# A two-block transformer kernel: narrower level matmuls, five reordered steps, and weight tiles placed 64 bytes further on

## The chip, the cores and the metric

One Trainium2 chip, one of its cores. The metric is the device time of one execution in microseconds (us). The kernel before takes 3259.83 us, the median of three runs (3259.44 to 3262.21).

## The reference, cut to what matters

256 tokens (`T`) of width 2048 (`D`) pass through four layers, all in float32. Each layer begins with a norm over the width and ends with a product that is added to the stream.

```python
x = hgrn2_layer(...)    # stage A, OA: h @ w_in (2048 x 8192), gated linear recurrence with 16 heads of 128,
                        #   head norm, silu gate, @ w_out
x = fox_layer(...)      # stage FG, F, OF: keys, values, queries, gate from 2048-wide products, causal softmax
                        #   with a forget bias, head norm, silu gate, @ w_out
                        # second block, stage X, C, OC:
proj = rmsnorm(x) @ w_in          # recurrence input, queries, latent keys/values, index queries and keys, 2 gates
y_rnn  = rg_lru(causal_conv(xr))  # per-channel linear recurrence
y_attn = dsa_attention(...)       # per query the 64 best keys by an index score, then softmax over them
x = x + (sigmoid(gr) * y_rnn + sigmoid(ga) * y_attn) @ w_o
                        # stage Q, U0..U3, V0..V3: a product-key expert layer over all 16384 experts
act = gelu(x @ u.T) * gate        # gate is zero but for the 128 chosen experts of a token
x = x + act @ v
return rmsnorm(x)
```

In the recurrence of stage A the mask inside a 128-token block is built from seven levels: at level l the block falls into pairs of halves of h = 2^l tokens, and the second half of each pair (queries) meets the first half (keys).

## The kernel before, in words

Everything is one program with a hand-written order on each engine. A weight matrix is cut into *units* of 128 output columns: one DMA of 1 MB from the SP queue into one of four `raw` slots, ScalarE copies it in two halves to `wh` (rounded to the fp32r format, L1049), VectorE writes `raw - wh` over `raw` as `wl` (`low_half`, `low_part`, L1512). TensorE then does 48 matmuls for a unit (`product`, L518 to L520): for each of 16 slices k the weights `wh[k]` against the high part `hh[k]` and the low part `hl[k]` of the stream, and `wl[k]` against `hh[k]`. In these the weight slice (128 columns, 512 bytes in a partition) is the *stationary* operand and the slice of the stream (256 columns, 1024 bytes) the *moving* one. In the profile's names the moving operand stands first: `bank<-hh,wh`. Keys and values of stage F use `kh` and `kl` in place of `hh` and `hl`.

In the value stages V0 to V3 it is the other way round: `ah` and `al`, the high and low parts of the activations, are stationary and the weights move, 512 columns at a time (L1018 to L1020). In stage C two small products use `uk_h`, `uk_l` as stationary and `ckv_h`, `ckv_l` as moving (L868 to L870), right after them `ckv` as stationary and `uv_h`, `uv_l` as moving (L876 to L878).

SBUF tensors are laid out one after another, each rounded up to 32 bytes. From the shapes the start addresses within a partition come out as follows (bytes): `hh` 16384, `hl` 32768, `kh` 141312, `ckv_h` 145408, all multiples of 1024; `wl` 49216 and `wh` 81984 onwards in steps of 8192, all 64 past a multiple of 1024; `uk_h` 153664 is 64 past one, `uv_h` 161984 is 192 past one; `ah` 194368 and `al` are 832 past one (320 past a multiple of 512).

The steps that the change touches:
- `a_levels` (L664 to L684) issues on TensorE for each of the seven levels four float32 matmuls of 128 stationary columns (`KL[l]`) by 64 moving columns (the second halves of `QL[l]`); the profile shows each float32 matmul as two. `a_masks` on VectorE (L1718 to L1738) takes the wanted squares out of PSUM into `AT`, with four masked copies per level.
- `out_projection` (L604) with `products_in_flight` (L579 to L602) begins the output products of a stage while the last head pair is still being finished: `count` units are computed up to slice 13, and at given points (unit, slice) the work of the last pair is put in: `f_values` (weigh the values) and `f_norm` (the head norm's sum, which waits for `osq_f` from ScalarE). The last two slices of those units come at the end. A raw slot is given back only when its unit is complete.
- In stage X VectorE sums the index scores of 16 heads (L1896) and in between splits weights (`low_part`).
- In the first head pair of stage C `select` (four rounds of max and replace) is called twice around the step that reads `ri_read`.
- `v_turns(2)` (stage V2) runs on VectorE for each unit: `act_low` (the low part of the activations for the next unit), two `low_half`, `gate` for the next block, and after the 16th and 32nd unit `add_experts`, which adds four PSUM banks to the stream. TensorE waits for these adds before it reuses a bank.

Of the kernel before, what the change touches and what calls it, by code (L numbers as in the profile page):

```python
# [24 lines left out]
P = 128  # L25
D = 2048
T = 256
KC = D // P
NT = T // P
# [6 lines left out]
LEVELS = 7  # L36
SC = P + T
# [12 lines left out]
BJ = 32  # L50
# [50 lines left out]
def program(nc, x_fm, prm_h, f_bias_h, w_in_a, w_out_a, w_fgate, w_kv, w_in_b, w_out_b, w_latent, w_ikey, w_iquery, w_in_c,  # L101
            rg_wa, rg_wx, w_uk, w_uv, w_out_c, w_q, keys1, keys2, peer_u, peer_v, fin_h, out):
    ctx = ExitStack()
    with ctx:
# [14 lines left out]
        qw = sb("qw", [P, 1])  # L119
        m = ExitStack()  # L120
# [12 lines left out]
        spare = sb("spare", [P, 16])  # L133
# [193 lines left out]
        frstd = sb_in(m, "frstd", [P, 40])[:, 0:NT]  # L327
# [180 lines left out]
        def _(eng):  # L508
# [155 lines left out]
            def a_levels(i):  # L664
# [9 lines left out]
                for l in range(LEVELS):  # L674
                    h = 1 << l
                    bank, at = (B[5 + l // 2], (l % 2) * T) if l < 6 else (B[3], 0)
                    if l == 6:
                        eng.wait_ge(s["gate_read"], i + 1)
                    for n in range(2 * NT):
                        last = eng.matmul(bank[:, at + n * (P // 2):at + (n + 1) * (P // 2)], KL[l][:, n * P:(n + 1) * P],  # L680
                                          halves(QL[l][:, n * P:(n + 1) * P], h)[:, :, 1, :], start=True, stop=True)
# [97 lines left out]
            out_projection("OF", "F", "C", 2, {(0, 6): (f_values,), (0, 12): (f_norm,)})  # L779
# [728 lines left out]
        def _(eng):  # L1508
# [209 lines left out]
            def a_masks(i, first, end):  # L1718
# [9 lines left out]
                for l in range(first, end):  # L1728
                    h, nb = 1 << l, P >> (l + 1)
                    bank, at = (B[5 + l // 2], (l % 2) * T) if l < 6 else (B[3], 0)  # L1730
                    dst = AT[:, :, :].rearrange("p n (b two r) -> p n b two r", two=2, r=h)[:, :, :, 1, :]
# [4 lines left out]
                    last = eng.drain()  # L1736
                if end == LEVELS:
                    last.then_inc(s["at_ready"], 1)  # L1738
# [148 lines left out]
            low_part(0, u + 9)  # L1887
            for n in range(IDX_HEADS):
                if n % 4 == 0 and n // 4 < 3:
                    low_part(0, u + 10 + n // 2)  # L1890
                    low_part(0, u + 11 + n // 2)
# [40 lines left out]
            def c_body(i, first, final=False):  # L1932
# [23 lines left out]
                low_part(i, u + 5)  # L1956
                if first:
                    select(TOPK // 16)
                eng.wait_ge(s["ri_read"], i + 1)
# [210 lines left out]
            def v_turns(b):  # L2170
# [4 lines left out]
                for n in range(BJ):  # L2175
# [4 lines left out]
                    if more:  # L2180
                        low_half(0, u, 0)
                    if gating:
                        gate(b + 1, 0, n, (b + 1, 0, n + 2) if n + 2 < BJ else None)
# [4 lines left out]
                    if n % (BJ // 2) == BJ // 2 - 1:  # L2188
                        add_experts(b, n // (BJ // 2))
# [106 lines left out]
```

## Time and profile before

| | |
|---|---|
| median of 3 runs | 3259.83 us (3259.44 to 3262.21) |
| the profiled execution's own time | 3263.68 us |
| its span in the trace | 3261.9 us |
| TensorE matmul busy | 3224.8 us, 99% |
| weight load busy | 3061.1 us, 94% |
| VectorE busy | 2334.3 us, 72% |
| ScalarE busy | 1656.7 us, 51% |
| granted TensorE clock, mean | 0.997 |
| DMA | 569.95 MB, mean 175 GB/s |

The span is the time from the first to the last instruction in the trace of one execution. A matmul's duration there includes its way through the array, so consecutive matmuls overlap; what a matmul costs in a stream is the distance from start to start, which is called *pitch* below.

### The profile page before, as it was taken

The page shows a single profiled execution, that of the slowest core. Times are in us where ns is not written, and L with a number is a line of the kernel's source. Part 1 is how long each engine was busy: PE and PEld are TensorE (multiplying, and loading weights), DVE is VectorE, ACT ScalarE, POOL GpSimd, SP SyncE. Part 2 cuts the span into 40 slices and gives each one's busy share as a digit, 9 for nine tenths or more (in the row PEclk, how much of TensorE's full clock was granted, in tenths as well). Part 3 has the DMA queues.
Part 4 walks back from the last instruction along what each step waited for, and adds up shares of the span by engine and source line. Part 5 has one row for each costly group of instructions (what it writes and reads, how often), then busy time and mean ns, then how long its engine had stood idle before and what let it go on. Part 6 is the DMA issues. An engine that isn't in the chain of part 4 may idle for free.

```text
span 3261.9 us, 62833 instructions
## 1 busy us (share of the span) xinstructions
PE 3224.8 (99%) x25256; PEld 3061.1 (94%) x25256; DVE 2334.3 (72%) x3775; ACT 1656.7 (51%) x2215; POOL 7.5 (0%) x27
## 2 busy tenths in 40 slices
PE   8999999999999999999999999999999999999998
PEld 7999999999999999999999999998899889987887
DVE  7767666654555676666668998985698658999865
ACT  5454544767674555656544434444444444444444
POOL 0000000000000000000000000000000000000000
PEclk9999999999999999999999999999999999999999
DMA  5444435444444455454555455555555555555554
GB/s 183 142 167 143 166 131 180 168 156 166 155 167 168 168 182 173 163 187 164 176 183 180 172 192 181 182 190 194 187 186 184 191 193 184 181 181 181 181 206 155
DMA packets 99095, 569.95 MB, mean 175 GB/s; under 512 B 9456, under 2 KB 30320, under 8 KB 31600
## 3 DMA queue, kind: packets, MB, share of 16 engines
q1 hardware_dynamic: 98928, 567.58, 49.6%
q8 instruction: 122, 2.00, 0.2%
q14 instruction: 45, 0.37, 0.0%
HBM read 565.45 MB, written 2.10 MB: 174 GB/s over the span
## 4 chain that ended last, share of the span: by engine, by line
PE 89%; DVE 8%; DVEq 1%; ACT 1%; issue 0%; DMA 0%; ACTq 0%; SPq 0%
PE bank L518 21%; PE bank L519 20%; PE bank L520 20%; PE bank L1018 6%; PE bank L1020 6%; PE bank L1019 6%; DVE wl L1512 2%; PE bank L680 2%; PE bank L944 1%; PE bank L622 1%; DVE hot_a L2096 1%; DVEq L2115 1%; PE bank L858 0%; PE bank L743 0%; PE bank L742 0%
## 5 line engine op out<-in xcount | busy, mean ns | idle before, releaser
L518 PE MATMUL bank<-hh,wh 128*128 128x256 f32 x5696 | 1612.0, 283 | 10.2 <-DVE hl L1545 9.0
L519 PE MATMUL bank<-hl,wh 128*128 128x256 f32 x5696 | 1582.6, 278 | 0.0
L520 PE MATMUL bank<-hh,wl 128*128 128x256 f32 x5696 | 1582.5, 278 | 0.0
L1512 DVE TENSOR_TENSOR wl<-raw,wh 128x1024 fp32r<-128x1024 f32 x1052 | 1253.8, 1221 | 413.7 <-ACT wh L1049 405.8
L1049 ACT ACTIVATE wh<-raw 128x1024 fp32r<-128x1024 f32 x1052 | 1052.1, 1050 | 316.2 <-DMA raw<-w_in_a 135.8
L518 PEld LDWEIGHTS bank<-hh,wh 128*128 128x128 f32 x5696 | 1074.0, 189 | 22.2 <-issue 12.5
L519 PEld LDWEIGHTS bank<-hl,wh 128*128 128x128 f32 x5696 | 1073.7, 189 | 7.3 <-issue 6.9
L520 PEld LDWEIGHTS bank<-hh,wl 128*128 128x128 f32 x5696 | 1073.3, 188 | 0.0
L1018 PE MATMUL bank<-wh,ah 128*128 128x512 f32 x1024 | 402.0, 393 | 1.3 <-DVE xT L2161 1.3
L1020 PE MATMUL bank<-wl,ah 128*128 128x512 f32 x1024 | 398.9, 390 | 0.0
L1019 PE MATMUL bank<-wh,al 128*128 128x512 f32 x1024 | 398.6, 389 | 0.0
L1018 PEld LDWEIGHTS bank<-wh,ah 128*128 128x128 f32 x1024 | 192.3, 188 | 40.8 <-DVE xT L2161 1.7
L1020 PEld LDWEIGHTS bank<-wl,ah 128*128 128x128 f32 x1024 | 192.2, 188 | 40.8
L1019 PEld LDWEIGHTS bank<-wh,al 128*128 128x128 f32 x1024 | 192.4, 188 | 39.1
L2096 DVE TENSOR_TENSOR hot_a<-iota_h,slotT 128x1024 f16<-128x1024 f16 x128 | 156.0, 1219 | 0.0
L518 PE MATMUL bank<-kh,wh 128*128 128x256 f32 x496 | 141.2, 285 | 0.0
L520 PE MATMUL bank<-kh,wl 128*128 128x256 f32 x496 | 138.4, 279 | 0.0
L519 PE MATMUL bank<-kl,wh 128*128 128x256 f32 x496 | 138.4, 279 | 0.0
L1464 ACT ACTIVATE ah<-act 128x512 fp32r<-128x512 f32 x64 | 40.4, 631 | 179.0 <-PE bank L1020 179.0
L2122 DVE TENSOR_TENSOR al<-act_odd,ah 128x512 fp32r<-128x512 f32 x64 | 44.3, 693 | 120.5 <-ACT ah L1464 120.5
L1449 ACT ACTIVATE act_odd<-bank 128x256 f32<-128x256 f32 (+1 forms) x64 | 24.6, 384 | 205.7 <-PE bank L520 205.7
L1464 ACT ACTIVATE ah<-act_odd 128x512 fp32r<-128x512 f32 x64 | 40.4, 632 | 173.0 <-PE bank L1020 171.8
(364 smaller groups left out, 2849.4 us busy)
## 6 DMA issues: line engine op xcount, KB each, us to landing
raw<-peer_u SPq DMA_DIRECT2D x128, 1024.0 KB, 4.9
raw<-peer_v SPq DMA_DIRECT2D x128, 1024.0 KB, 4.9
raw<-w_in_c SPq DMA_DIRECT2D x64, 1024.0 KB, 4.9
raw<-w_in_a SPq DMA_DIRECT2D x63, 1024.0 KB, 4.9
raw<-w_kv SPq DMA_DIRECT2D x32, 1024.0 KB, 4.9
raw<-w_in_b SPq DMA_DIRECT2D x32, 1024.0 KB, 4.9
raw<-w_out_a SPq DMA_DIRECT2D x16, 1024.0 KB, 5.0
raw<-w_out_b SPq DMA_DIRECT2D x16, 1024.0 KB, 4.9
```

The source lines that it names most:

```text
L518: eng.matmul(out, h_[:, k, :], high[:, k, :], start=(k == 0), stop=False)
L519: eng.matmul(out, h_[:, k, :], low[:, k, :], start=False, stop=False)
L520: last = eng.matmul(out, low_rows(c, k), high[:, k, :], start=False, stop=(k == KC - 1))
L680: last = eng.matmul(bank[:, at + n * (P // 2):at + (n + 1) * (P // 2)], KL[l][:, n * P:(n + 1) * P], halves(QL[l][:, n * P:(n + 1) * P], h ...
L1018: eng.matmul(bank[:, :], a_h, w_h, start=first, stop=False)
L1019: eng.matmul(bank[:, :], a_l, w_h, start=False, stop=False)
L1020: last = eng.matmul(bank[:, :], a_h, w_l, start=False, stop=final)
L1049: eng.activation(high_half(c, half), raw_half(c, half), ACT.Copy).then_inc(hi_ready, 1)
L1464: eng.activation(ah[c % 2][:, :, :], acts[b % 2][:, 2 * c:2 * c + 2, :], ACT.Copy).then_inc(s["ah_ready"], 1)
L1512: eng.tensor_tensor(low_half_out(c, half), raw_half(c, half), high_half(c, half).bitcast(F32), ALU.subtract).then_inc(lo_ready, 1)
L2096: eng.tensor_tensor(hot_a[c % 2][:, :, :], iota_h[:, :].unsqueeze(1).broadcast_to(ka), slotT[:, 0, tt].unsqueeze(2).broadcast_to(ka), ALU. ...
L2122: eng.tensor_tensor(al[c % 2][:, :, :], acts[b % 2][:, 2 * c:2 * c + 2, :], ah[c % 2][:, :, :].bitcast(F32), ALU.subtract).then_inc(s["al_ ...
```

## The change

It has seven edits. `NARROW = 5`: levels 5 and 6 of `a_levels` use only the columns that are wanted. `spare` moves in front of `raw`: `wl` and all `wh` start 64 bytes later, at 128 past a multiple of 1024; `iota`, `prm`, `ident` and `ones` move with them, and from `tri` on every address is as before. `frstd` gets 16 more floats: `ah`, `al` and what follows start 64 bytes later too, at 896 past a multiple of 1024 (384 past a multiple of 512). The other four change the order of work.

```diff
+NARROW = 5
@@ addresses
+        spare = sb("spare", [P, 16])        # now ahead of raw, wl, wh
-        spare = sb("spare", [P, 16])        # was behind rg_c
-        frstd = sb_in(m, "frstd", [P, 40])[:, 0:NT]
+        frstd = sb_in(m, "frstd", [P, 56])[:, 0:NT]
@@ a_levels, TensorE
                     for n in range(2 * NT):
-                        last = eng.matmul(bank[:, at + n * (P // 2):at + (n + 1) * (P // 2)], KL[l][:, n * P:(n + 1) * P],
-                                          halves(QL[l][:, n * P:(n + 1) * P], h)[:, :, 1, :], start=True, stop=True)
+                        if l < NARROW:
+                            eng.matmul(...)      # as before
+                        else:
+                            for a in range(0, P, 2 * h):
+                                eng.matmul(bank[a:a + h, at + n * (P // 2) + a // 2:at + n * (P // 2) + a // 2 + h],
+                                           KL[l][:, n * P + a:n * P + a + h], QL[l][:, n * P + a + h:n * P + a + 2 * h], start=True, stop=True)
@@ a_masks, VectorE
+                    if l >= NARROW:
+                        level = bank[:, at:at + T].rearrange("p (n t) -> p n t", n=2 * NT)
+                        for a in range(0, P, 2 * h):
+                            eng.tensor_copy(AT[a:a + h, :, a + h:a + 2 * h], level[a:a + h, :, a // 2:a // 2 + h])
+                        continue
@@ TensorE, end of stage F
-            out_projection("OF", "F", "C", 2, {(0, 6): (f_values,), (0, 12): (f_norm,)})
+            out_projection("OF", "F", "C", 3, {(0, 6): (f_values,), (1, 0): (f_norm,)})
@@ VectorE, stage X
+            lows_at = {0: (10, 11), 4: (12, 13), 8: (14,), 12: (15,)}
             for n in range(IDX_HEADS):
-                if n % 4 == 0 and n // 4 < 3:
-                    low_part(0, u + 10 + n // 2)
-                    low_part(0, u + 11 + n // 2)
+                for c in lows_at.get(n, ()):
+                    low_part(0, u + c)
@@ VectorE, first pair of stage C
-                low_part(i, u + 5)
                 if first:
                     select(TOPK // 16)
+                low_part(i, u + 5)
@@ VectorE, v_turns
+                    if gating and n == BJ // 2 - 1:
+                        add_experts(b, 0)
                     if gating:
                         gate(b + 1, 0, n, (b + 1, 0, n + 2) if n + 2 < BJ else None)
...
-                    if n % (BJ // 2) == BJ // 2 - 1:
+                    if n == BJ - 1 or n == BJ // 2 - 1 and not gating:
                         add_experts(b, n // (BJ // 2))
```

## Rows read from the trace of the kernel before

**Rows 1.** The page: span, and each engine's busy us, share of the span, instructions.

```profile
span 3261.9 us, 62833 instructions
PE 3224.8 (99%) x25256; PEld 3061.1 (94%) x25256; DVE 2334.3 (72%) x3775; ACT 1656.7 (51%) x2215; POOL 7.5 (0%) x27
```

**Rows 2.** Stretches of 30 us: each engine's busy us (instructions), clock, DMA share, GB/s.

```profile
1010.00:1040.00 30.00, 30.00 (x257) 30.00 (x256) 18.13 (x23) 12.89 (x15) 0.00 (x0) 1.00 0.56 199
1640.00:1670.00 30.00, 30.00 (x267) 30.00 (x266) 17.92 (x23) 11.99 (x14) 0.00 (x0) 1.00 0.52 179
```

**Rows 3.** Groups by line, count | busy us, mean ns: 1010 to 1040, 1640 to 1670, whole run.

```profile
L519 PE MATMUL bank<-hl,wh 128*128 128x256 f32 x86 | 24.2, 281 | 0.0
...
L519 PE MATMUL bank<-hl,wh 128*128 128x256 f32 x89 | 24.6, 276 | 0.0
...
L519 PE MATMUL bank<-hl,wh 128*128 128x256 f32 x5696 | 1582.6, 278 | 0.0
```

**Rows 4.** Timeline of TensorE, a later pair of stage C: start, duration.

```profile
1253.44 0.28 PE L870 MATMUL bank<-ckv_h,uk_l 128*128 128x256 f32 x1
...
1255.91 0.28 PE L870 MATMUL bank<-ckv_h,uk_l 128*128 128x256 f32 x1
...
1256.27 0.28 PE L878 MATMUL bank<-uv_h,ckv_l 128*128 128x256 f32 x1
...
1258.77 0.28 PE L518 MATMUL bank<-hh,wh 128*128 128x256 f32 x1
...
1259.47 0.28 PE L518 MATMUL bank<-hh,wh 128*128 128x256 f32 x1
```

**Rows 5.** A 30 us stretch of stage V0, matmuls of L1019 alone.

```profile
2200.00:2230.00 30.00, 17.15 (x45) 8.27 (x45) 1.00 0.58 206
```

**Rows 6.** Timeline of TensorE: the levels of one head pair; one gate turn, f16.

```profile
77.50 6.36 PE L680 MATMUL bank<-QL,KL 128*128 128x64 f32 x56
...
2101.22 0.41 PE L944 MATMUL bank<-gates_b,hot_a 128*128 128x64 f16 x8
```

**Rows 7.** Timeline of TensorE around index scores, which use 64 of 128 rows.

```profile
1166.79 0.28 PE L520 MATMUL bank<-hh,wl 128*128 128x256 f32 x1
1167.00 1.69 PE L807 MATMUL bank<-kiT,qi 64*128 64x128 f32 x16
1168.62 0.39 PE L518 MATMUL bank<-hh,wh 128*128 128x256 f32 x1
```

**Rows 8.** Timeline of TensorE, starts of OA and OF: waits in brackets.

```profile
489.49 0.39 PE L518 MATMUL bank<-hh,wh 128*128 128x256 f32 x1 [0.43 <-DVE wl L1512]
...
993.70 1.13 PE L622 MATMUL bank<-osq_f,ones 128*128 128x512 f32 x2 [0.75 <-ACT osq_f L1240]
...
1000.83 0.38 PE L588 MATMUL bank<-hh,wh 128*128 128x256 f32 x1 [0.35 <-DVE hl L1570]
```

**Rows 9.** Timeline of VectorE and TensorE, stage X and first pair of stage C.

```profile
1168.79 2.36 DVE L1512 TENSOR_TENSOR wl<-raw,wh 128x1024 fp32r<-128x1024 f32 x2 [6.00 <-ACT wh L1049]
1171.24 6.77 DVE L1896 SCALAR_TENSOR_TENSOR iscore<-relu,kw,iscore 128x128 f32<-128x128 f32 x16
...
1184.35 2.76 DVE L1950 SCALAR_TENSOR_TENSOR xc<-bank,prm,xc 128x255 f32<-128x255 f32 x6
...
1191.89 2.36 DVE L1512 TENSOR_TENSOR wl<-raw,wh 128x1024 fp32r<-128x1024 f32 x2 [2.28 <-ACT wh L1049]
...
1187.41 1.03 PE L858 MATMUL bank<-xc,wa 128*128 128x256 f32 x4
...
1221.15 0.87 PE L628 MATMUL bank<-ident,prob_c 128*128 128x128 f32 x6 [2.70 <-DVE prob_c L1816]
```

**Rows 10.** Timeline of VectorE and TensorE, middle of stage V2.

```profile
2979.83 0.42 DVE L2111 SCALAR_TENSOR_TENSOR g_sum<-bank,g_low 128x256 f32<-128x256 f32 x1
...
2983.87 2.48 DVE L2161 TENSOR_TENSOR xT<-bank,xT 128x512 f32<-128x512 f32 x4
...
2984.61 0.50 PE L1018 MATMUL bank<-wh,ah 128*128 128x512 f32 x1 [1.29 <-DVE xT L2161]
```

More of the change, by code:

```diff
@@ L679, in a_levels @@
                     for n in range(2 * NT):
-                        last = eng.matmul(bank[:, at + n * (P // 2):at + (n + 1) * (P // 2)], KL[l][:, n * P:(n + 1) * P],
-                                          halves(QL[l][:, n * P:(n + 1) * P], h)[:, :, 1, :], start=True, stop=True)
+                        if l < NARROW:
+                            eng.matmul(bank[:, at + n * (P // 2):at + (n + 1) * (P // 2)], KL[l][:, n * P:(n + 1) * P],
+                                       halves(QL[l][:, n * P:(n + 1) * P], h)[:, :, 1, :], start=True, stop=True)
+                        else:
+                            for a in range(0, P, 2 * h):
+                                eng.matmul(bank[a:a + h, at + n * (P // 2) + a // 2:at + n * (P // 2) + a // 2 + h],
+                                           KL[l][:, n * P + a:n * P + a + h], QL[l][:, n * P + a + h:n * P + a + 2 * h], start=True, stop=True)
                 for j in range(2):
@@ L1735, in a_masks @@
                                             .rearrange("p (b r) -> p b r", r=h))
-                    last = eng.drain()
+                    eng.drain()
                 if end == LEVELS:
-                    last.then_inc(s["at_ready"], 1)
+                    eng.drain().then_inc(s["at_ready"], 1)
             def a_body(i, first):
```

## The prediction

> **What bounds the kernel now.** I read the page first. TensorE's matmuls cover 99% of the span and VectorE 72% [rows 1], so a microsecond counts only where TensorE waits or where its own work gets shorter or longer. The list of waits then showed that TensorE waits little: a few places of 0.5 to 3 us, three of which the change aims at [rows 8 to 10]. So the rest is the pitch of a matmul, and there the stretches of 30 us show something unexpected. Both stretches hold nothing but the same three lines at the same granted clock, 1.00 (the 2.4 GHz level), with the DMA and VectorE doing nearly the same, but one has 257 matmuls and the other 267 [rows 2]. About 2.4 of each count are matmuls that only reach into the stretch, so the pitch is 30/254.6 = 117.8 ns in the one and 30/264.6 = 113.4 ns in the other. I call them long and short pitch. The groups show the same as a duration: 281 ns in the stretch of 257, 276 in that of 267, 278 over the whole run [rows 3]. So some (278-276)/5 = 2/5 of these matmuls go at the long pitch (3/10 to 5/10 with the rounding). There are 5696 of each of three lines with `hh`, and 496 more of each with `kh`, together 18,576. At the long pitch: 7,400, at 4.4 ns, so it costs 33 us of the span (25 to 41). Matmuls at the short pitch: 11,100.
>
> Is it a matter of addresses, which the change moves? One place speaks for it [rows 4]. In stage C the key product (stationary 64 past a multiple of 1024, moving on one) goes at (1255.91-1253.44)/21 = 117.6 ns; then without a pause the value product (stationary on a multiple of 512, moving 192 past one of 1024) at (1258.77-1256.27)/22 = 113.6 ns; then, again without a pause, the ordinary product (64 past, and on one) at (1259.47-1258.77)/6 = 117 ns. The switch follows the operands. Against it: ordinary products with the very same placement also go at the short pitch in one of the two stretches of rows 2. So the placement of 64 allows both, and something else, the timing at which a run of matmuls is entered, chooses. The new placement of 128 occurs nowhere in this trace.
>
> **The change part by part.** Against the profiled execution: 3263.68 us, of which the span is 3261.9.
>
> *Narrow levels.* Levels 5 and 6 are 16 of the 56 records in 6.36 us [rows 6], less about 0.16 us for the last one's way out: 0.111 us each, 1.77 us a pair. After it there are 8 matmuls of 32 by 32 columns and 4 of 64 by 64, which makes 16 + 8 = 24 records, and three changes of the array's shape. No row shows a matmul with fewer than 128 stationary columns. Upper end: each of the 24 costs 0.111 as now, 2.66. Lower end: 0.030 each, the start-to-start of the f16 matmuls (eight within 0.41 us, the last one's 0.19 included) [rows 6], 0.72. The nearest shape change is that to 64 rows and back: 1167.00-1166.79 is 0.21 where 0.12 is usual, and the first product behind it lasts 0.39 instead of 0.28 [rows 7]. So some 0.1 each way; three are 0.3, and 0.6 if such a change costs double. Between the ends I take 0.03 for the 16 and 0.055 for the 8, half of 0.111 for half the columns: 0.48 + 0.44 + 0.5 = 1.42, a gain of 0.35 a pair and 2.5 us over eight pairs, rounded down. Ends: 0.72 + 0.3 (1.02 a pair) gives -6 us, 2.66 + 0.6 (3.26) gives +12. VectorE's masks get about 1 us shorter a pair, beside TensorE: nothing. The Trainium skill ("TensorE: Matmul & The Clock Gate", LDWEIGHTS) has the load time go with the column count, and "TensorEngine Tiling (Array Packing)" (Key Properties) says that a change of the tiling mode drains the array; the first alone would be an estimate of 27 ns a load for 32 columns, hence 16 x 0.027 + 8 x 0.053, a gain of 0.9 us a pair before the drains. No row here has such a load.
>
> *Start of OF.* The head norm waits 0.75 us for `osq_f`, and the last pair's `hl` another 0.35, about 0.5 with the issue behind it [rows 8]. Now six more matmuls lie ahead of the norm (24 rather than 18): 0.68 us of the first wait is filled. Behind the norm come 84 matmuls, about 9.7 us, for a chain that took 1000.83-993.70 = 7.1 us: the second wait goes. Gain 1.2. But with three units in flight the first raw slot comes free only after 42 more matmuls. OA runs that way already, and there TensorE waits 0.43 us for `wl` at its fifth unit [rows 8], 0.6 with the restart. I book that as the price: net -0.7.
>
> *Stage X and the first pair of C.* VectorE waits 2.28 us for `wh` before a `low_part`, and `select` now fills that: -2.28 on its chain [rows 9]. The `low_part` of unit 15 used to start at 1168.79, before the last index scores were there, and now comes behind four of them. They can begin at some point between 1168.8 and 1171.24; I take 1170.6, as VectorE had found none to work on in the six idle microseconds before. Then 6.77 us of scores and 2.3 of low parts end at 1179.7 instead of 1178.0: +1.7 on the same chain (0 to 2.3 by the two ends). That also moves the convolution (`xc`, now ready at 1187.1): 1188.8, while TensorE wants it at 1187.41 [rows 9]. A new wait of 1.4 us stands there, but it is paid out of the wait of 2.70 for the transposes, which ends the same stretch: TensorE resumes there at 1221.15 - 2.28 + 1.7 = 1220.6. Net -0.6. Queued behind the new wait is only the rest of TensorE's own list; ScalarE's sigmoids follow it and have 4 us to spare.
>
> *`add_experts` earlier.* TensorE waits 1.29 us for the first add, 1.5 with the restart. VectorE gets to that point at 2979.83 and adds at 2983.87, 4.0 us later [rows 10]. Moved ahead, the first add would be done before TensorE wants it: -1.4. Behind it the gate comes 2.5 us later, and so do the pairs for the spread of unit 17 and `act_low`; the unit in between gives TensorE 24 x 0.227 = 5.4 us of work, which just covers them. If it doesn't, half of this comes back.
>
> *Addresses of the weights.* Bounds by the two pitches: all go at the short one, -33 us; all at the long one, 11,100 x 4.4 ns = +49. Nearest is neither end: the same mixture, chosen anew at each entry. I take 0 and keep ±8 for the choice. One sentence of the Trainium skill speaks against any effect: "SBUF — State Buffer" (Who interferes with whom) gives TensorE two read ports of its own, one for the moving and one for the loaded operand, and says that it never waits on anyone; by it this term is exactly 0. The two pitches at one clock are not explained by it.
>
> *Addresses of `ah` and `al`.* Both operands of the value stages move by 64 bytes, so their distance stays 256 modulo 512. The pitch there is 30/45/3, some 0.227 us at 512 columns [rows 5], twice the short 113.4. I take 0.
>
> **Sum**: -2.5 - 0.7 - 0.6 - 1.4 = -5.2 us, 3258.5 for the profiled execution. The median of the runs lies 3.85 below that execution: 3254.6, so 3255.
>
> **Rivals.**
>
> *The long pitch vanishes.* If 128 bytes keep the two reads apart as the value product's placement does [rows 4], the 33 us go as well: 3255 less 25 to 33, about 3226. For it: the only place where the pitch switches without a pause. Against: that place differs from the new one in both operands.
>
> *The long pitch spreads* (the other side). If 128 is the worse distance, matmuls at the short pitch now fall to 117.8 ns. It costs more than the 5.2 us of the other edits as soon as 1,200 of the 11,100 fall. Half of them: +25, 3280; all: 3304. For it: a stretch at the long pitch, once entered, lasts for hundreds of matmuls (the 30 us of rows 2 are wholly one or the other). Against: nothing but that the present mixture is no extreme.
>
> *The value stages catch it.* Their moving tile is now 64 past a multiple of 128 and comes to lie on one, like `hh`, whose products know the long pitch. 3 x 1024 matmuls of 512 columns at twice 4.4 ns: +27, 3282. Against: they load weights for half the time only.
>
> *The edits don't do what they say*: the narrow records cost the full 0.111. +14 against the sum, 3269.
>
> **How the numbers follow.** Likeliest, 0.42: mixture as before, 3255, own range 3244 to 3267. Slow pitch vanishes 0.25, spreads 0.24, value stages 0.05, narrow matmuls at full price 0.04. What a measurement of this kernel tells from no change is about 0.2%, 6.5 us: 3253.3 to 3266.4 is the same. The likeliest case lies on that border and gives 0.18 faster, 0.20 the same, 0.04 slower; with the others faster 0.43, same 0.20, slower 0.37. The range runs from 3223 into the case of spreading, to 3290.
>
> **What would show it.** The mean duration of L519 is the gauge of the pitch: 278 now, 276 if the long pitch is gone, 281 if it is everywhere. L1019 tells the value stages. The L680 group and the narrow one together should take 5.9 to 6.1 us a pair. The wait for `osq_f` should fall under 0.2 us and a wait for `wl` of 0.4 appear some 12 us behind it; L858 should wait 1.4 us for `xc` and L628 under 1 us for `prob_c`; the wait of 1.29 us for `xT` should be gone. I am wrong if L519's mean moves by more than 1 ns, or if a new wait of over 1.5 us stands anywhere.

## The result and the profile after

The changed kernel takes 3325.17 us (median of 4 runs, 3323.74 to 3325.8) against 3261.02 for the kernel before (4 runs, 3259.44 to 3262.56): a ratio of 1.0195, 95% interval 1.0181 to 1.0209. It is slower by 64 us, where 3255 was forecast and the range ended at 3290.

The page of the changed kernel:

```profile
span 3322.6 us, 62913 instructions
PE 3291.6 (99%) x25320; PEld 3127.1 (94%) x25320; DVE 2331.6 (70%) x3735; ACT 1656.2 (50%) x2215; POOL 7.8 (0%) x27
```

TensorE's matmuls are busy for 67 us more than in [rows 1] and its weight loads for 66; the other engines stay within 3 us. Its matmuls by line (the lines moved down: L518, L519, L520 of before are L519, L520, L521, and L1018 to L1020 are L1024 to L1026):

```profile
L519 PE MATMUL bank<-hh,wh 128*128 128x256 f32 x5680 | 1629.1, 287 | 8.6 <-DVE hl L1551 8.2 <-DVE wl L1518 0.4
L521 PE MATMUL bank<-hh,wl 128*128 128x256 f32 x5680 | 1600.4, 282 | 0.0
L520 PE MATMUL bank<-hl,wh 128*128 128x256 f32 x5680 | 1599.7, 282 | 0.0
...
L1025 PE MATMUL bank<-wh,al 128*128 128x512 f32 x1024 | 398.3, 389 | 0.0
```

The gauge of the prediction, 278 ns in [rows 3], stands at 282: above the 281 of the long pitch, and 4 ns off where more than 1 was to be the sign of being wrong. Two stretches of 30 us that hold nothing but these products (columns: PE, PEld, DVE, ACT, POOL busy us, clock, DMA share, GB/s):

```profile
1040.00:1070.00 30.00, 30.00 (x256) 30.00 (x255) 19.15 (x25) 13.05 (x16) 0.00 (x0) 1.00 0.55 187
1640.00:1670.00 30.00, 30.00 (x256) 30.00 (x255) 18.83 (x25) 14.14 (x18) 0.00 (x0) 1.00 0.51 176
```

Both have 256 matmuls at a granted clock of 1.00, where [rows 2] had 257 in one and 267 in the other. From one start to the next, over the whole trace and with pauses left out, the products with `hh` stand at 118.68 ns (before: 114.76, made of 113.4 and 117.8). In a product at 113.4 all steps are 113 or 114 ns, at 117.8 they are 117 to 119; at 118.7 they go 120, 119, 115, 118 and 121 or 122 in turn. I call 16 slices k of three matmuls a product; there are 392 of them. In the kernel before, 268 are short and 124 long; in the changed kernel none is at either pitch: those with `hh` are all at this third one, those with `kh` at 119.5 ns. The value products stay at 227.2 ns (before 227.2).

The list of TensorE's waits (us in total, times, longest):

```profile
PE bank L519 <- DVE hl L1551: 8.2, 8, 3.7
PE bank L567 <- ACT sq L1066: 6.6, 1, 6.6
...
PE bank L864 <- issue: 0.5, 1, 0.5
PE bank L1024 <- DVE al L2133: 0.5, 1, 0.5
PE bank L519 <- DVE wl L1518: 0.4, 2, 0.2
```

They sum to 19.4 us against 25.2 before: `osq_f` (0.7), `prob_c` (2.7), `xT` (1.3) are gone; 0.5 for L864 and 0.5 for `al` are new. The levels of a head pair, which took 6.20 us from the first start to the next group in the kernel before, take 84.43 - 78.94 = 5.49:

```profile
78.94 4.58 PE L682 MATMUL bank<-QL,KL 128*128 128x64 f32 x40
83.45 1.05 PE L686 MATMUL bank<-QL,KL 128*32 128x32 f32 x24
84.43 0.71 PE L689 MATMUL bank<-QL,KL 128*128 128x128 f32 x4
```

The account of the span, with the steps counted over the whole trace: 17,240 steps with `hh` by 3.92 ns are +67.6 us, 1561 with `kh` by 3.59 (115.91 to 119.50) +5.6, waits -5.8, levels 8 x 0.71 = -5.7: +61.7, and 60.7 was measured.

### The profile page after: what moved, and what is told of

Its sections match the earlier page's. It is cut to its first block, busy times and chain, and to the rows that moved or that the text cites. A ratio compares the mean times of both kernels' runs of the same rounds, so it can differ in the third digit from the quotient of the medians.

```text
span 3322.6 us, 62913 instructions
## 1 busy us (share of the span) xinstructions
PE 3291.6 (99%) x25320; PEld 3127.1 (94%) x25320; DVE 2331.6 (70%) x3735; ACT 1656.2 (50%) x2215; POOL 7.8 (0%) x27
## 4 chain that ended last, share of the span: by engine, by line
PE 96%; DVE 2%; ACT 1%; DMA 1%; DVEq 0%; issue 0%; ACTq 0%; SPq 0%
PE bank L519 22%; PE bank L521 22%; PE bank L520 22%; PE bank L1024 7%; PE bank L1026 7%; PE bank L1025 7%; PE bank L950 1%; PE bank L682 1%; PE bank L623 1%; PE bank L864 0%; DVE wl L1518 0%; PE bank L629 0%; PE bank L749 0%; PE bank L748 0%; PE bank L896 0%; DVE oT L1541 0%
## 5 line engine op out<-in xcount | busy, mean ns | idle before, releaser
L519 PE MATMUL bank<-hh,wh 128*128 128x256 f32 x5680 | 1629.1, 287 | 8.6 <-DVE hl L1551 8.2
L521 PE MATMUL bank<-hh,wl 128*128 128x256 f32 x5680 | 1600.4, 282 | 0.0
L520 PE MATMUL bank<-hl,wh 128*128 128x256 f32 x5680 | 1599.7, 282 | 0.0
L519 PEld LDWEIGHTS bank<-hh,wh 128*128 128x128 f32 x5680 | 1071.5, 189 | 20.2 <-issue 12.9
L520 PEld LDWEIGHTS bank<-hl,wh 128*128 128x128 f32 x5680 | 1071.8, 189 | 7.4 <-issue 7.0
L521 PEld LDWEIGHTS bank<-hh,wl 128*128 128x128 f32 x5680 | 1071.1, 189 | 0.0
L1024 PE MATMUL bank<-wh,ah 128*128 128x512 f32 x1024 | 401.9, 392 | 0.5 <-DVE al L2133 0.5
L1026 PE MATMUL bank<-wl,ah 128*128 128x512 f32 x1024 | 398.9, 390 | 0.0
L1026 PEld LDWEIGHTS bank<-wl,ah 128*128 128x128 f32 x1024 | 192.2, 188 | 40.3
L1024 PEld LDWEIGHTS bank<-wh,ah 128*128 128x128 f32 x1024 | 192.3, 188 | 40.1 <-DVE al L2133 0.9
L519 PE MATMUL bank<-kh,wh 128*128 128x256 f32 x496 | 143.4, 289 | 0.0
L520 PE MATMUL bank<-kl,wh 128*128 128x256 f32 x496 | 140.7, 284 | 0.0
L521 PE MATMUL bank<-kh,wl 128*128 128x256 f32 x496 | 140.6, 284 | 0.0
L1455 ACT ACTIVATE act<-bank 128x256 f32<-128x256 f32 (+1 forms) x64 | 24.7, 386 | 216.4 <-PE bank L521 216.4
```

The costliest lines, as they stand in the source:

```text
L519: eng.matmul(out, h_[:, k, :], high[:, k, :], start=(k == 0), stop=False)
L520: eng.matmul(out, h_[:, k, :], low[:, k, :], start=False, stop=False)
L521: last = eng.matmul(out, low_rows(c, k), high[:, k, :], start=False, stop=(k == KC - 1))
L1024: eng.matmul(bank[:, :], a_h, w_h, start=first, stop=False)
L1026: last = eng.matmul(bank[:, :], a_h, w_l, start=False, stop=final)
L1455: eng.activation(acts[b % 2][:, ds(i * PER_PAIR + c, 1), :].rearrange("p o t -> p (o t)"), B[DOT_BANK[b] + c % 2][:, 0:T], ACT.Gelu).then_ ...
```

## The experiments

Theory P says that the place of the weights against the activations, modulo some power of two, sets the pitch. I write *distance* for the byte address of the tile that is loaded minus that of the tile that is streamed: of the weights minus `hh` for the main products (64 before, 128 after), of `ah` minus `wh` for the value products.

**e1: both address edits taken back; e2: the weights' edit alone; e3: the narrow levels alone.**

```diff
 e1, against the changed kernel
-        spare = sb("spare", [P, 16])      # ahead of raw
+        spare = sb("spare", [P, 16])      # behind rg_c
-        frstd = sb_in(m, "frstd", [P, 56])[:, 0:NT]
+        frstd = sb_in(m, "frstd", [P, 40])[:, 0:NT]
 e2, against the kernel before: spare ahead of raw
 e3, against the kernel before: NARROW = 5, with its two branches
```

> The changed kernel with both address edits taken back (weight tiles 64 bytes off again, value activations too), all its other edits kept. Theory P (the addresses of the weights set the pitch of the main matmuls): the weight matmuls go back to the mixture of before, 2 in 3 at 113.3 ns from start to start and 1 in 3 at 117.8, L519's mean to 281 ns or below, and the other edits keep their 8 to 10 us: about 3251 us, 74 us below the changed kernel. Rival E (another edit, the narrow matmuls that use part of the array above all, brings the long pitch in every run after them): the pitch stays at 118.7 ns and the time at about 3325 us.

> The kernel before with the 64-byte spare tile allocated ahead of the weight tiles, and nothing else: the weight tiles stand 128 bytes off the activations in place of 64, all other tiles where they were (the value activations too). Theory P: pitch 118.7 ns in every main product, 18,000 matmuls x 3.95 ns = 71 us more than before, about 3332 us. Rival E: no change of the pitch, 3261 us.

> The kernel before with the narrow products of levels 5 and 6 alone. Theory P: each of the eight pairs of stage F gains the 0.71 us by which a pair's level rows differ between the two kernels, 5.7 us in all, 3255 us, with the mixture of pitches as before (it may be dealt out anew to the tiles, some 10 us to either side). Rival E: the pitch goes to 118.7 ns behind the first narrow product, 3320 us.

(The levels are in stage A; the stage F of e3's expectation is a slip.)

Measured: e1 3253.92 (ratio to before 0.9975, 0.9965 to 0.9985), e2 3338.3 (1.0236, 1.0219 to 1.0253), e3 3256.97 (0.9984, 0.9974 to 0.9993). Theory P holds in all three and rival E in none. In e1 a stretch at either pitch is back (1640 us and 1870 us, columns as above), with 129 long products of 392:

```profile
1640.00:1670.00 30.00, 30.00 (x267) 30.00 (x266) 18.07 (x23) 11.90 (x14) 0.00 (x0) 1.00 0.54 179
1870.00:1900.00 30.00, 30.00 (x257) 30.00 (x256) 28.55 (x89) 12.71 (x18) 0.00 (x0) 1.00 0.51 179
```

e2 costs 6 us more than the 71 expected, and its lines show where: the main products are at 118.70 ns as after the change, but the value products, whose stationary tile stayed while the weights moved, went from 227.2 to 229.0 ns:

```profile
L519 PE MATMUL bank<-hl,wh 128*128 128x256 f32 x5696 | 1604.3, 282 | 0.0
L1018 PE MATMUL bank<-wh,ah 128*128 128x512 f32 x1024 | 405.4, 396 | 1.0 <-DVE xT L2161 1.0
```

L1018 was 393 in the kernel before and in e1. 3035 steps by 1.8 ns are 5.4 us: that is what moving `ah` and `al` along is worth.

**e4: the pitch by itself.** Products of three factors over two buffers, shifted by a number of bytes each; no transfer and no other engine beside them.

```python
for s, m in PAIRS:                  # bytes: loaded tile, streamed tile
    eng.matmul(B[0][:, :], ones[:, :], sq[:, :], start=True, stop=True)
    product(s, m, 0); product(s, m, 1)
    for _ in range(4):
        eng.matmul(B[0][:, 0:P], ones[:, :], ones[:, :], start=True, stop=True)
    product(s, m, 0); product(s, m, 1)
```

> The pitch by itself; the whole computation of the reference is left out. Products of 48 matmuls (a 128 x 128 stationary tile, 256 moving columns, sixteen k, the same three factors a k) over two buffers shifted by so many bytes: stationary 0, 32, 64, ... 448 against activations at 0, then activations at 64 to 512 against several. No transfer and no other engine runs beside them. Theory P1: the pitch goes by the difference of the two addresses within 1024 bytes or less: 113 ns at 64, 118.7 ns at 128, and the rest of the list shows the rule. Rival P2: the pitch goes by something else that runs beside the matmuls (writes of VectorE and ScalarE, the transfers into the weight buffers), so all rows here show the same pitch. Rival P3: the pitch is chosen anew where a run of matmuls starts, so the four products of one row differ among themselves.

Windows of 10 us inside the first entry of (0,0), (64,0), (192,0), (320,0), and of both entries of (0,192); columns PE, clock, DMA share, GB/s:

```profile
41.05:51.05 10.00, 10.00 (x86) 1.00 0.01 2
90.29:100.29 10.00, 10.00 (x87) 1.00 0.01 2
188.51:198.51 10.00, 10.00 (x87) 1.00 0.00 0
237.65:247.65 10.00, 10.00 (x90) 1.00 0.00 0
359.23:369.23 10.00, 10.00 (x90) 1.00 0.00 0
371.33:381.33 10.00, 10.00 (x87) 1.00 0.01 2
```

The pitch from start to start, each over 95 steps, put in order by the distance modulo 256 (this order was found afterwards, with e9 to e12):

```
distance mod 256   pitch, ns                       entries
0                  119.9 to 120.0                  10 of 10
32, 160            118.3; 119.9
96                 118.7, 117.3
128                118.6 to 120.0                  4 of 4
64                 113.4 or 117.8                  7 short, 7 long of 14
192                117.8                           10 of 10
```

P2 (something beside the matmuls makes the pitch) falls: all levels stand here with the rest of the core idle. P1 and P3 are both right: the distance sets which pitches there are, and at some distances the entry chooses between two. In this bench 113.4 comes at 64 alone; at 96 and 128 there are two pitches as well (118.7 and 117.3, 118.6 and 120.0), but all above 117.

**e5: the four tiles shifted apart; e6: what turns one pitch into the other.** e5 moves high and low tiles one by one, e6 puts a small matmul between two products.

> The whole computation of the reference is left out. Products of 48 matmuls as in the main kernel (stationary high with moving high, stationary high with moving low, stationary low with moving high, for sixteen k), the four tiles shifted each by its own number of bytes, each set entered four times: behind one fp32 matmul of 512 columns, and behind one, two and three of 128. Then products of 48 with 512 moving columns. From the bench before (a distance of 64 bytes modulo 128 gave 113.4 or 117.8 ns, 0 gave 119.9, 32 gave 118.3): theory D (the distance between the tile being loaded and the tile being streamed decides, matmul by matmul) expects the sets in which one of the two pairs of tiles is 0 apart between 113.4 and 119.9 in proportion, and no set below 113. Theory S (the state is chosen at the entry) expects both 113.4 and 117.8 among the four entries of the 64-byte set and one number for each set that is 0 apart. Rival: only multiples of 64 matter and 4, 16, 32, 48 bytes behave as 0. For 512 columns: 227 at 0 and 229 to 233 at 64, as the changed kernel and the bench before had it.

> The whole computation of the reference is left out. Products of 48 matmuls with the weights 64 bytes off; a row enters once behind an fp32 matmul of 128 columns (117.8 ns in the bench before) and once behind one of 512 (113.4 to 113.7), then puts a small matmul of 8 to 192 moving columns, or of fewer loaded columns, or an fp32 one, between the first and the second product and again before the third. Theory S (which of the two pitches a run takes hangs on how the stream of loads and the stream of moving columns are shifted against each other at its start, in steps of a few columns): some lengths turn 117.8 into 113.4 and others leave it, with the first row (nothing between) the same in all three products. Rival R (the state hangs on what the fp32 matmuls leave behind): no small matmul of the weights' own kind changes it, only the fp32 ones do.

e5: with all tiles 64 apart, 113.7, 117.8, 117.8, 113.3 behind the four entries; in the other seven mixtures of 0 and 64, 116.7 to 119.9 and no entry at 113; at 4, 16 and 32 bytes 118.2 to 118.4, at 48 117.7 to 117.8 with one entry at 123.3, at 80 118.7 to 118.8, at 112 119.9 to 120.0. So theory D's sum over the pairs of tiles fails (one pair off costs the whole short pitch), and the rival that only multiples of 64 matter fails too. Value products: 227.2 ns at distance 0, 228.9 at -64 (192), 233.3 at 64. e6: a matmul of 32 loaded and 16 moved columns turned the pitch each time, from either side (duration of the middle line in the three products behind one entry, with such a matmul ahead of the second and of the third):

```profile
L80 PE MATMUL bank<-m_all,s_all 128*128 128x256 f32 x14 | 3.9, 281 | 0.0
L80 PE MATMUL bank<-m_all,s_all 128*128 128x256 f32 x14 | 3.9, 276 | 0.0
L80 PE MATMUL bank<-m_all,s_all 128*128 128x256 f32 x14 | 3.9, 281 | 0.0
```

Behind 128 loaded and 192 moved columns, and behind two matmuls of 128 and 16, all eight products came out short. Behind one matmul of 128 loaded and 8 to 96 moved columns, six lengths, all 24 products came out long, also where the one ahead had been short. Rival R of e6 falls; theory S stands in the bench.

**e7, e8: markers in the kernel, misplaced.**

```diff
+                if len(counted) - 1 in MARKED:
+                    eng.matmul(out[0:32, 0:16], w[:, 0, 0:32], high[:, 0, 0:16], start=True, stop=True)
```

> The kernel of e1_addresses_back (3253.9 us) with one small matmul (32 columns loaded, 16 moved, into the place that the product then overwrites) ahead of the first matmul of each of 68 runs of products that stood at 117.8 ns in its trace; those runs hold 129 of 392 products. Theory S (the pitch of a run is chosen by how it starts, and such a matmul shifts the start): if each of them turns its run to 113.3, 129 x 48 x 4.4 ns = 27 us less, less 68 x 0.03 us = 2 us for the matmuls themselves: 3229 us. As the short pitch also turned into the long one in the bench, runs behind a marked one may turn the other way: each product that does gives back 0.21 us, so 3240 to 3250 us is the likely result of a part that turns. Rival R (the marker does nothing at an entry, since the fp32 matmul or the wait ahead of it decides): the same dealing as in e1, 3254 to 3256 us.

> The kernel of e1_addresses_back with a marker (32 columns loaded, 16 moved) at three places only, each between two products inside a run at 117.8 ns, where the bench turned 117.8 into 113.3: in the last products of stage F (12 of them, the marker behind the first), in the three of the value projection behind them (marker behind the first) and in the 22 of the latent queries (marker behind the first). Theory S: 11 + 2 + 21 = 34 products fall to 113.3 ns, 34 x 48 x 4.4 ns = 7.2 us less than e1, 3247 us, if the runs behind them keep their dealing. Rival R (a marker as in e7 does not turn a run): 3254 us.

e7 3263.8 (1.0018, 1.0007 to 1.0029), e8 3251.38 (0.9979, 0.9969 to 0.999). Neither tests the sum of its theory. I had numbered the products as the trace shows them, but the program counts calls, and a loop over seven pairs is written once: the program has 216 calls for 392 products, so e7's markers ran seven times at some places and others never, and of e8's three two ran, at 1997 and 2113 us, and one stood at no call. The trace of e7 still tests the marker itself. It ran 84 times, of these 23 times between two matmuls of the products, and there it turned the pitch every time: 8 from 117.8 to 113.3 ns, 15 from 113.3 to 117.8, as in the bench. The middle line ahead of the marker at 1638.59 us, behind it, and behind the next at 1644.36:

```profile
L530 PE MATMUL bank<-hl,wh 128*128 128x256 f32 x15 | 4.1, 276 | 0.0
L530 PE MATMUL bank<-hl,wh 128*128 128x256 f32 x14 | 3.9, 281 | 0.0
L530 PE MATMUL bank<-hl,wh 128*128 128x256 f32 x15 | 4.1, 276 | 0.0
```

e8 told something else: up to 1997 us it does the same as e1, yet of the seven later pairs of stage A the first two products are long in seven pairs in e1 and in four in e8. So one and the same code is dealt out differently from one execution to another, and over the whole run 107 products are long in e8 and 129 in e1: 22 x 48 x 4.4 ns = 4.6 us. That is a third of the spread between runs of one kernel (3253.5 to 3266.8 for the kernel before, beside e7 to e15); that the dealing makes this spread is likely, but one trace of each kernel doesn't show it.

**e9: weights at 192; e12: the same with the tiles behind them kept in place modulo 256; e11: weights at 320.**

```diff
 e9, against the changed kernel
-        spare = sb("spare", [P, 16])
+        spare = sb("spare", [P, 32])
-        frstd = sb_in(m, "frstd", [P, 56])[:, 0:NT]
+        frstd = sb_in(m, "frstd", [P, 72])[:, 0:NT]
 e12, against e1
+        ahead = sb("ahead", [P, 32])       # ahead of raw
+        behind = sb("behind", [P, 32])     # ahead of tri
-        frstd = sb_in(m, "frstd", [P, 40])[:, 0:NT]
+        frstd = sb_in(m, "frstd", [P, 72])[:, 0:NT]
 e11, against e1
+        ahead = sb("ahead", [P, 64])       # ahead of raw
```

> The changed kernel with its weight tiles 192 bytes off in place of 128, and its value activations 64 bytes further too, so that their distance from the weights stays. Theory M (the distance counts modulo 128 bytes): 192 is as 64, the main products stand at 113.3 and 117.8 ns again in some mixture (two to one gives 114.8), and the time is that of e1_addresses_back, 3254 us, 10 us to either side by the mixture. Rival N (64 bytes is a distance of its own, every other costs): 118 ns or more, 3310 us or more.

> The kernel of e1_addresses_back with the weights at 192 bytes modulo 256, the tiles behind them moved by 256 (nothing modulo 256) and the value activations moved so that they stay 0 from the weights modulo 256: e9 without its side effects, where the value activations landed 192 from the weights (233 ns) and the activations of the second norm 128. Theory Q: main products at 117.3 to 117.8 as in e9, value products back at 227 ns: 18,800 x 2.6 to 3.0 ns = 49 to 56 us above e1, 3303 to 3310 us. If the value products stay at 233 ns, distance modulo 256 is not their rule: 3321 to 3328 us.

> The kernel of e1_addresses_back with 256 bytes of padding ahead of the weight tiles: weights at 320 bytes modulo 1024 in place of 64, and all tiles behind them 256 further too, so that only the distance of the weights from hh and hl changes (64 to 320). Read modulo 256, all runs so far fall in order: 64 gives 113.3 or 117.8 ns by the entry, 192 mostly 117.8, 0 gives 119.9, 128 gives 118.7. Theory Q (modulo 256): 320 is as 64, a mixture of 113.3 and 117.8 with the value products at 227: 3244 to 3260 us. Theory Q' (modulo 512 or more, since the bench had both its entries at 320 short): nearly all runs at 113.3, 129 x 48 x 4.4 ns = 27 us less: 3227 us. Rival (any move off 64 costs): 3310 us or more.

e9 3327.27 (1.021, 1.0193 to 1.0227), e12 3302.72 (1.013, 1.0113 to 1.0147), e11 3251.65 (0.9976, 0.9966 to 0.9985). e9's time refutes theory M, modulo 128: 3254 us was forecast by it. One part of it stays, the two pitches (below). Its expectation also had a slip: the tiles behind the weights moved by 64 too, so `ah` went 128 bytes and its distance from `wh` rose from 0 to 64 modulo 256 (the expectation of e12 counts it the other way round, 192). What it measured fits the bench at that distance: value products at 233.3 ns, 3037 x 6.1 = 18.5 us. e12 takes this out. A stretch of main products and one of value products in e12:

```profile
1640.00:1670.00 30.00, 30.00 (x257) 1.00 0.55 193
2260.00:2290.00 30.00, 30.00 (x134) 1.00 0.54 195
```

The first is at 117.8 ns, with 368 of 392 products long; the second at 227 ns again. The other 24 products of e12, and 30 in e9, are at 113.3 ns. So 192 has the same two pitches as 64, only dealt out otherwise, though the bench had all its ten entries at 192 long. In e9 a run of twelve such products covers this stretch:

```profile
1040.00:1070.00 30.00, 30.00 (x267) 1.00 0.53 181
```

At 128 no product of the three kernels that have it is short. e11 has 119 long products and the time of e1. The whole-run steps side by side:

```
kernel           distance mod 256    main, ns   long of 392   value distance, ns   us
before           64                  114.76     124           0    227.2           3261.0
e1               64                  114.77     129           0    227.2           3253.9
e11              320 = 64            114.70     119           0    227.2           3251.7
e12              192                 117.49     368           0    227.2           3302.7
e9               192                 117.43     362           64   233.3           3327.3
changed kernel   128                 118.68     all, 3rd      0    227.2           3325.2
e2               128                 118.70     all, 3rd      192  229.0           3338.3
```

Modulo 256 (theory Q) puts kernels and bench in one order, but for the few short products at 192. That 64 and 192 differ at all is clearer in the value products, 233.3 against 229.0 ns. Q', nearly all short at 320, failed by 24 us.

**e10: the wide form of levels 5 and 6 at the changed kernel's addresses.**

```diff
-NARROW = 5
+NARROW = 7
```

> The changed kernel with levels 5 and 6 back in their wide form (the narrow products taken out), at the addresses of the changed kernel, where no run has two pitches. The level rows of the two traces, 6.20 us a pair before and 5.49 after, give 8 x 0.71 = 5.7 us: 3331 us against the changed kernel's 3325. The prediction's own price was 2.5 us: 3328. If the rest of a narrow product (its switches, VectorE's copies) eats it: 3325.

3330.5 (1.0219, 1.0202 to 1.0236), 5.3 us above the changed kernel. With the pitch the same in both (118.68 ns), this is what the narrow form gains by itself: 0.66 us a pair by the times. The trace agrees: 0.71 us up to the next group, of which 0.05 come back at the first wide matmul behind it (213 ns from start to start where 165 were usual).

**e13, e14, e15: can the start of a run be steered?** Twenty places, this time numbered by the program. The expectations count 57 runs of them, the traces of e13 and e14 show 50. e15 takes at 15 places the marker of e13, at two the pair of e14, and none at three: 41 runs.

```diff
 e13
+                    eng.matmul(out[:, 0:192], w[:, 0, :], high[:, 0, 0:192], start=True, stop=True)
 e14: two of
+                        eng.matmul(out[:, 0:16], w[:, 0, :], high[:, 0, 0:16], start=True, stop=True)
```

> The kernel of e1_addresses_back (3253.9 us) with a marker of 128 loaded and 192 moved columns ahead of the first product of the runs that start at 117.8 ns in most of five traces: 20 places in the program, run 57 times with their loops. In the bench all five such markers between two products were followed by 113.3 ns, from either pitch. Theory S: these runs go to 113.3, 79 products x 48 x 4.4 ns = 16.7 us less, and the markers cost 57 x 0.09 = 5 us: 3242 us, and some 50 long products of 392 in the trace instead of 107 to 129. Rival R (at an entry what stands before the run decides): the same dealing, 3254 + 5 = 3259 us.

> The same places with two matmuls of 128 loaded and 16 moved columns as the marker, which in the bench were also followed by 113.3 ns in four of four cases, at 0.14 us each. Theory S: 3254 - 16.7 + 57 x 0.14 = 3245 us. Rival R: 3262 us.

> The kernel of e1_addresses_back with the markers of e13 where the trace of e13 showed 113.3 ns behind them (ahead of products in stages X, C and the queries), the pair of short matmuls of e14 at two places where only that one worked (first product of a pair in stage A's loop, last product of a pair in stage C's), and none at the others. Theory S: the trace shows some 60 long products of 392 (e13 had 76 with its own dealing elsewhere), and of e13's time go 23 markers of 0.09 us or more (2 us) and 19 products x 0.21 us less 14 x 0.14 us (2 us): 3246 us. Rival R (a place turns by its history, not by its marker): the dealing of e13 or worse, 3250 to 3255 us.

e13 3250.28 (0.9971, 0.9962 to 0.9981), e14 3262.5 (1.0013, 1.0003 to 1.0022), e15 3255.16 (0.9984, 0.9975 to 0.9993). Where a marker works, it works place by place. The two products of stage C's loop behind the gate's matmuls and behind the value projection were long in all 70 cases of five traces (before, e1, e3, e8, e11) and short in all 28 of e13 and e15. One of them, the middle line in e1, e13 and e15:

```profile
L520 PE MATMUL bank<-hl,wh 128*128 128x256 f32 x13 | 3.7, 281 | 0.0
```

```profile
L530 PE MATMUL bank<-hl,wh 128*128 128x256 f32 x14 | 3.9, 276 | 0.0
```

```profile
L531 PE MATMUL bank<-hl,wh 128*128 128x256 f32 x13 | 3.6, 276 | 0.0
```

Behind other matmuls (the levels of stage A, the scores of stage F, the transposes of stage C) the same marker left the run long, 23 of 23; the pair of short ones turned two of these three places, in 13 of 14 cases in e14 and in 13 of 14 in e15, but in e14 it left the run behind the value projection long in 7 of 8. In e15, 40 of 41 marked starts are short.

In sum, though, little is won, and the traces show two reasons. A marker costs more than was booked: by the time from the matmul ahead to the fourth one behind, 0.11 us for the one of 192 columns and 0.21 to 0.23 for the pair (0.09 and 0.14 booked), which makes 6 us in e15. And a turned run can turn the next one: in stage C's loop of e15 the product behind the transposes became short in all seven pairs, and the three behind the weighing of the values that follows, short in e1, became long in all seven. These two runs differ in pitch in 71 of 72 cases of nine traces (before, e1, e3, e7, e8, e11, e13 to e15), in three of which (e7, e14, e15) a marker had turned the first. So the pitch of a run seems to hang on that of the run ahead too, and not only on the matmuls between. So 91 products are long where 60 were expected. 91 against 129 gives 8 us for 6 us of markers, and e15 is no lower than e1 (3255.16 against 3253.92, intervals that overlap). In e14 and e15 the eight products of the first pair, which stand ahead of every marker, are all long, where e1 has seven of them short. What turned those stays open. e13 has the lowest time of all, but its interval overlaps those of e1 and e11.

## Why the prediction was wrong, by its own steps

**What bounds the kernel.** Right in the main: the waits changed by 6 us and the pitch made the rest. But "a few places of 0.5 to 3 us" misreads the list of waits: of its 25.2 us, one wait is 6.7 (`sq`, L566) and one 3.7 (`hl`). The change touches neither. The count of long matmuls at 2/5 was a little high: 124 of 392 products, a third.

**Addresses of the weights: the step that failed.** "Nearest is neither end: the same mixture, chosen anew at each entry. I take 0." The bounds were taken from the two pitches that the trace shows, on the silent premise that a new placement can only redistribute them. It has a pitch of its own, 118.7 ns, beyond the upper bound: +73 us where the ends were -33 and +49 and 0 was booked. The mixture of 113.4 and 117.8 belongs to the distances 64 and 192 modulo 256 (at 192 one product in 13 to 16 is short, e9 and e12); 128 and 0 have no short products (e2, e4, e10). e2 shows that this edit alone costs more than the whole change lost (77 us against 64). What in the engine ties the pitch to the distance no run shows.

**The evidence of rows 4.** I read the turn between key and value product as the operands' doing, in favour of a placement that keeps the short pitch. In the changed kernel, with these tiles at the same addresses, the key product goes at 113.3 ns and the value product at 117.8, the other way round, and in e1 the first pair does so too and the seven later ones not. Both are 64 modulo 256 apart, in opposite roles; the turn was one of entries. The sentence against it, that something at the entry chooses, was right, and e6 and e13 show it.

**The rule of the Trainium skill.** By the Trainium skill, "SBUF — State Buffer" (Who interferes with whom), TensorE's two read ports are independent and it never waits on anyone; so the term would be 0. The measurement decides against that outcome for these float32 tiles: 113.4, 117.8, 118.7 and 119.9 ns at a clock of 1.00, with nothing else running in e4. Whether the two reads wait for each other is not shown.

**The rivals.** Spreading had the right sign and the right cause, a worse distance, but not the pitch and so too small a price: "all" at 3304 was the long pitch everywhere, as e12 nearly has it (3302.7); the third pitch adds another 20 us. The vanishing of the long pitch and the full price of narrow matmuls are refuted. The value stages did not catch it, but not since they load weights for half the time only: moved against each other they lose 1.8 ns (e2) or 6.1 (e9). They kept their pitch as their distance was kept, which is what the term for `ah` and `al` said.

**Narrow levels.** Mechanism right, size off: 5.3 to 5.7 us gained, 2.5 booked. The 24 records take 0.98 us, 1.08 with the change of shape ahead of them (205 ns where 112 are usual), against the 1.42 estimated. In the trace the 16 small ones start in pairs 32 ns apart, 16 ns each where 30 were taken, which is 0.22 of the 0.34 us; the 64-column ones stand 58 apart (55 taken); the changes of shape add some 0.36 in all, not 0.5.

**Start of OF.** As booked: the waits for `osq_f` and `hl` are gone; the trace shows a step of 0.53 us from start to start where the fifth unit begins (1033.1 us), 19 us behind the norm's sum, where a `wl` wait of 0.4 was named some 12 us behind it; the list puts no wait there.

**Stage X and the first pair of C.** The net was near (-0.6 booked; in e1 the two waits are 1.6 us where `prob_c` was 2.7), the parts were not. L864 waits 0.5 and not 1.4, and L629 not at all. VectorE no longer waits 2.28 us for `wh`, but 7.47 for ScalarE's `relu` of the ninth of the 16 heads:

```profile
1191.05 3.27 DVE L1907 SCALAR_TENSOR_TENSOR iscore<-relu,kw,iscore 128x128 f32<-128x128 f32 x8 [7.47 <-ACT relu L1332]
```

This trace has all its products longer, so its slack is wider; in e1, at the old pitch, L864 waits 0.9 and L629 0.7. The price named for `xc` was half a microsecond too high there.

**`add_experts` earlier.** Right: 1.3 for `xT` gone, 0.5 for `al` new here, and no such wait in e1.

**The sum without the weights.** -5.2 forecast. e1 measures it: a ratio of 0.9975 to the kernel before, -8.2 us (-4.9 to -11.4), 3 us of the difference being the size of the narrow gain. The edits of order are worth about 3 us together, 3253.92 against e3's 3256.97, where 2.7 were booked; the intervals of the two overlap, and both hold a dealing of their own.

## What to carry to other kernels

Where TensorE is busy for 99% of the span at full clock, count matmuls in equal windows before anything else: two counts for the same lines are two pitches, and the addresses are to be suspected. Treat the placement of loaded against streamed tiles as a parameter with its own measured table, and bound a placement that the trace doesn't show by a bench and not by the placements that it shows. Before gaps and orders of 1 us are tuned, write down each tile's address modulo 256, as any tile allocated ahead shifts all behind it.

## What the runs showed of the hardware

- Back-to-back float32 matmuls of 256 columns with 128 loaded have at least four pitches at one granted clock of 1.00: 113.4, 117.8, 118.7 and 119.9 ns, by the distance of the two SBUF tiles modulo 256 bytes. At 64 and at 192 there are two, 113.4 and 117.8, at 192 mostly the long one; either can be held for hundreds of matmuls (e1, e9, e12).
- With 512 columns the best of the distances tried is another: 227.2 ns at 0 (e5, every kernel but e2 and e9), 229.0 at 192 (e2, e5), 232.5 at 128 (e4), 233.3 at 64 (e4, e5, e9).
- Which of the two is taken depends on the matmuls directly ahead of the run, and at one place it was the opposite of the run before in 71 of 72 cases; one of 32 loaded and 16 moved columns inside a run turns it, in the bench (e6) and 23 times of 23 in the kernel (e7). Even so, the same code is dealt out differently in two executions, by some 20 of 392 products.
- Matmuls of 32 by 32 that use different column tiles start 6 and 25 ns apart in turn, 16 ns each; those of 64 by 64 every 58 ns; the change from the one to the other adds about 0.15 us, the entry from 128 columns and the return to them 0.09 each.
